# SyncE paces its expert weight loads: a granule's second transfer waits for the granule two places in front

## The reference

```python
def moe_swiglu(h, w_router, wg, wu, wd):
    logits = (h @ w_router).astype(jnp.float32)
    top_v, top_i = lax.top_k(logits, TOP_K)
    top_p = jax.nn.softmax(top_v, axis=-1)
    gates = jnp.sum(jax.nn.one_hot(top_i, N_EXPERTS, dtype=jnp.float32) * top_p[..., None], axis=-2)
    act = jax.nn.silu(jnp.einsum('bnd,edf->bnef', h, wg)) * jnp.einsum('bnd,edf->bnef', h, wu)
    act = act * gates.astype(h.dtype)[..., None]
    return jnp.einsum('bnef,efd->bnd', act, wd)
```

## Time and profile before

| | us |
|---|---|
| median of 3 runs | 1703.03 (1701.0 to 1705.19) |
| the profiled execution, its device time | 1703.7 |
| its span in the profile | 1701.9 |
| PE busy in the span | 1555.7 (91%) |
| SP's hardware queue | 195712 packets, 390.64 MB |
| mean traffic over the span | 254 GB/s |

### The profile page before, as it was taken

The page is one execution under the profiler, slowest core; times in us unless marked ns, Lnnn a source line. Parts: engine busy times, 40 slices in busy tenths (PEclk is TensorE's granted clock), DMA queues, the critical chain, the costliest instruction groups (busy, mean ns, idle before and its releaser), DMA issues.

```text
span 1701.9 us, 24840 instructions
## 1 busy us (share of the span) xinstructions
PE 1555.7 (91%) x9206; PEld 1034.7 (61%) x9207; DVE 760.2 (45%) x1236; ACT 555.3 (33%) x965; POOL 88.5 (5%) x109
## 2 busy tenths in 40 slices
PE   4798989999999799898878899999999989999795
PEld 1684567788888487467623577677566655655332
DVE  0483776433332655576610443333445534434225
ACT  0432454333332343361200333333244433334101
POOL 2010002200000011000100000000000000000002
PEclk8899999999999899999789999999999999999897
DMA  9245534944432623640999978887699999999992
GB/s 347 102 138 174 195 127 165 347 146 140 149 116 82 223 99 128 214 170 25 358 364 377 346 280 297 331 291 263 238 376 392 393 391 380 379 394 381 391 352 95
DMA packets 206624, 432.20 MB, mean 254 GB/s; under 512 B 11880, under 2 KB 52840, under 8 KB 206224
## 3 DMA queue, kind: packets, MB, share of 16 engines
q1 hardware_dynamic: 195712, 390.64, 63.3%
q0 software_dynamic: 7712, 29.05, 4.8%
q10 hardware_dynamic: 3056, 10.62, 1.8%
HBM read 409.55 MB, written 20.71 MB: 253 GB/s over the span
## 4 chain that ended last, share of the span: by engine, by line
issue 47%; PE 40%; DVE 6%; DMA 5%; ACT 2%; SPq 0%; POOL 0%; DVEq 0%; ACTq 0%; POOLq 0%
PE ps L2052 27%; PE ps L1984 3%; DMA small<-y_rows,row_at 2%; PE ps L2146 2%; DMA gu_ring<-in_w_ada 1%; PE ps L2111 1%; DMA d_ring<-in_w_ffn_down 1%; PE ps L2124 1%; PE ps L1987 1%; DVE gu_ring_parts L1320 1%; PE ps L1996 1%; PE ps L2008 1%; DVE smax L1412 1%; PE ps L2224 0%; PE ps L2598 0%
## 5 line engine op out<-in xcount | busy, mean ns | idle before, releaser
L2052 PE MATMUL ps<-d_ring_parts,scratch_parts 128*128 128x512 f32 (+1 forms) x444 | 171.8, 387 | 14.0 <-DVE hT_parts L1326 9.2
L2454 PE MATMUL ps<-ring,hT 128*64 128x512 f32 (+1 forms) x512 | 113.0, 585 | 19.1 <-issue 10.9
L2052 PE MATMUL ps<-gu_ring_parts,scratch_parts 128*128 128x512 f32 (+1 forms) x336 | 128.6, 383 | 0.0
L2052 PE MATMUL ps<-d_ring_parts,hT_parts 128*128 128x512 f32 (+1 forms) x312 | 119.2, 382 | 0.0
L2460 PE MATMUL ps<-ring,hT 128*32 128x256 f32 x1760 | 116.4, 382 | 3.0 <-issue 1.5
L1873 DVE TENSOR_TENSOR cst<-cst,ps 128x256 f32<-128x256 f32 (+2 forms) x89 | 32.7, 368 | 193.0 <-ACT cst L1159 193.0
L1184 ACT ACTIVATE qkv_parts<-ring 128x1024 fp32r<-128x1024 f32 x102 | 103.1, 1050 | 13.1 <-issue 13.1
L2052 PEld LDWEIGHTS ps<-d_ring_parts,scratch_parts 128*128 128x128 f32 x444 | 84.7, 191 | 32.2 <-issue 9.3
L2052 PE MATMUL ps<-gu_ring_parts,o_parts 128*128 128x512 f32 x264 | 103.3, 391 | 0.0
L1167 ACT ACTIVATE cst<-ps 128x128 f32<-128x128 f32 (+1 forms) x51 | 16.0, 315 | 235.3 <-PE ps L2476 225.9
L2454 PEld LDWEIGHTS ps<-ring,hT 128*64 128x64 f32 x512 | 36.1, 144 | 83.2 <-issue 68.4
(11 more groups left out here) (403 smaller groups left out, 3147.3 us busy)
## 6 DMA issues: line engine op xcount, KB each, us to landing
ring<-in_w_moe_gate SPq DMA_DIRECT2D x176, 512.0 KB, 10.4
ring<-in_w_moe_up SPq DMA_DIRECT2D x176, 512.0 KB, 11.3
ring<-in_w_moe_down SPq DMA_DIRECT2D x176, 512.0 KB, 10.0
gu_ring<-in_w_ada SPq DMA_DIRECT2D x48, 1024.0 KB, 7.4
gu_ring<-in_w_in SPq DMA_DIRECT2D x16, 1024.0 KB, 7.2
gu_ring<-in_w_ffn_gate SPq DMA_DIRECT2D x11, 1024.0 KB, 5.5
gu_ring<-in_w_ffn_up SPq DMA_DIRECT2D x11, 1024.0 KB, 8.1
d_ring<-in_w_ffn_down SPq DMA_DIRECT2D x11, 1024.0 KB, 10.0
```

The source lines that it names most:

```text
L2052: ins = pe.matmul(out, a, w, start=(start and n == 0), stop=(stop and n == 2))
L2454: ins = pe.matmul(ps[64 * j:64 * j + 64, bank, 0:2 * f].rearrange("p (a f) -> p a f", a=2), hT[:, kc, col:col + 64], wt[:, :, f * j:f * j ...
```

## The change

`IN_FLIGHT` is 2. In the loop, the first transfer of granule `pos` is issued as before; the second is issued only when granule `pos - 2` has landed in full (for `pos` 0 and 1 that is granule 31 or 32 of the turn before). In front of the loop, a granule's first transfer already waits for the granule two places earlier in the order of issue, and that order is written out in the list `first`; the waits for `ada_expanded` and `stored` stay where they were in it.

```diff
+IN_FLIGHT = 2
...
-            def load_granule(experts, pos):
+            def load_granule(experts, pos, pace=lambda: None):
...
                                      ).then_inc(landed, 16)
+                        if a == 0:
+                            pace()
...
                         sp.dma_start(half_view(ring, pos, f), w_moe_down[0, e][r0:r0 + P, :]).then_inc(landed, 16)
+                        if f == 0:
+                            pace()
...
+            def paced(t, pos, ahead=0):
+
+                if pos >= IN_FLIGHT:
+                    sp.wait_ge(ring_landed[pos - IN_FLIGHT], t * 32 + (32 * ahead + 32))
+                else:
+                    sp.wait_ge(ring_landed[pos - IN_FLIGHT + GRANULES], t * 32 + 32 * ahead)
+
+            first = list(range(1, 10)) + [0] + list(range(10, AHEAD))
             sp.wait_ge(out_mm, 12)
-            for pos in range(1, 10):
-                load_granule((0, 0), pos)
-            sp.wait_ge(ada_expanded, 32)
-            load_granule((0, 0), 0)
-            sp.wait_ge(stored, 128)
-            for pos in range(10, AHEAD):
+            for n, pos in enumerate(first):
+                if n >= IN_FLIGHT:
+                    sp.wait_ge(ring_landed[first[n - IN_FLIGHT]], 32)
+                if pos == 0:
+                    sp.wait_ge(ada_expanded, 32)
+                if pos == 10:
+                    sp.wait_ge(stored, 128)
                 load_granule((0, 0), pos)
...
                     freed(t, pos - AHEAD)
-                    load_granule(now, pos)
+                    load_granule(now, pos, lambda: paced(t, pos))
...
                     freed(t, pos + GRANULES - AHEAD)
-                    load_granule(then, pos)
+                    load_granule(then, pos, lambda: paced(t, pos, 1))
...
                 freed(NE - 1, pos - AHEAD)
-                load_granule(now, pos)
+                load_granule(now, pos, lambda: paced(NE - 1, pos))
```

## The result

The changed kernel takes 1715.74 us (median of 6 runs, 1710.56 to 1727.42) where the kernel before took 1702.01 us beside it (1696.62 to 1705.19). The ratio is 1.0099, with a 95% interval of 1.0071 to 1.0126. The forecast was 1703.5 us in a range up to 1711, with 0.16 for slower. So it was wrong, and the rival that names bubbles in the load stream was the one that came. The profiled execution has a span of 1716.5 us against 1701.9.

What follows compares the result with a forecast made beforehand. PE and the load stream were taken to bound the expert phase in turn. 1703.7 + 0 (SP instructions) + 0 (queue depth) + 0.5 (SP pauses) = 1704.2, less 0.7 for this execution: 1703.5 us, range 1696.5 to 1711; nothing measurable 0.72.

Steps and rivals of the forecast that it cites:

- the rival that names bubbles in the load stream: Second transfers in the stretches that count lose time: 0.1 us a granule gives 1710 us, 0.4 gives 1728; chance 0.16.
- What bounds the kernel: Expert phase: PE bounds 1000 to 1226 us; elsewhere the transfer engines are never out of work, DMA share 0.94 to 1.04.
- Instructions on SP: New waits in SP's issue stream, at most about 0.2 us each: SP needs 1.34 us of a granule's 2.71, cost nothing.
- The depth of the queue: At a second transfer's release, three transfers (4.05 us) cover 2.65 us of start, completion and wait: cost nothing.
- the rival's "for": Argument for bubbles: the 16 engines don't finish together, so the cover of 4.05 us is thinner for all but the slowest.
- The row on which the zero rested: Ring transfer issued at 1179.09 with three on their way landed 1.4 us behind the one before: taken as no loss.
- How many granules count: A delay moves PE only in 885 to 923 (some 13 granules) and 1226 to 1369 (some 49): 62 granules.
- The hiding: Last stretch: PE waits 5.3 us for DVE behind POOL's chain of gathers, so the first few us of delay are hidden.
- SP's pauses: Top of a turn, SP loads table values for 3.05 us: 0.3 us too much at about two places, 0.5 us in all.
- In front of the loop: Stricter pace, 2.7 us of cover against 2.65; a loss of some us by 881 is hidden by the hole there.
- The other queues: ACT's and POOL's transfers and code fetches get quicker: five gathers gain 1.55 us each, 7.8 us, 1696 us; chance 0.12.
- What would show it: Ring landings of 5 to 7 us, no long SP issues, about 387 GB/s; wrong if GB/s fall by 2% or more.

Runs made afterwards that it cites:

- All waits with none binding: The changed kernel with IN_FLIGHT 8 instead of 2, so every wait is executed and none holds anything back: 1701.98 us, ratio 1.0005.
- one ahead: The changed kernel with IN_FLIGHT 1, so one transfer is on its way when a landing lets the next go: 1989.91 us, ratio 1.1693.
- 3 ahead: The change itself against the kernel before: three transfers are on their way when a landing lets the next go; 1715.74 us, ratio 1.0099.
- two ahead: The changed kernel, IN_FLIGHT 2, wait moved in front of both transfers, so two are on their way at a release: 1762.58 us, ratio 1.0362.
- five: The changed kernel with IN_FLIGHT 3, wait still between the two transfers, so five are on their way at a release: 1700.57 us, ratio 0.9992.
- four ahead: The changed kernel, IN_FLIGHT 3, wait moved in front of both transfers, so four are on their way at a release: 1702.89 us, ratio 1.0013.
- the run with every third granule: The changed kernel, but only every third granule waits two places back, the others three: 1709.12 us, ratio 1.0051.

## Why the prediction was wrong

**What bounds the kernel** was read rightly. The two limits, and where each rules, are the same after, and the loss came through the stream in the stretches with a DMA share near 1.

**Instructions on SP: right.** All waits with none binding gave a ratio of 1.0005.

**The depth of the queue: the step that failed.** The forecast set the cover of 4.05 us against 2.65 us and took nothing. The 2.65 us hold for the slowest of the 16 engines, and one ahead shows it (median 3.9 us a granule against 4.0 by this sum). But the others are up to 1.9 to 2.9 us in front, so they run out of work with 3 ahead. The forecast named this in the rival's "for" and set it aside with "the slowest engine, which sets the landings, always has its three transfers". That would be enough if an engine that runs out simply gave up its lead. The packets show that it doesn't: some of those that follow a moment with too little under way take up to ten times the usual 84 ns. If I add the lead to what must fit, the sum is 2.65 + 1.9 to 2.9 = 4.6 to 5.6 us. Three ahead (4.05) and two (2.7) lose, five (6.75) don't, and four (5.4) stand on the edge and lose nothing that can be measured. That is what the table shows. The step from lead to slow packets is read from the traces; no run changed the lead by itself, so it is argued and not shown alone. It fits the table, but it doesn't say why most granules lose nothing with three ahead; the instruction transfers, which take about 1 us on their queue, are a likely part of that, untested. Nor does it fit the run with every third granule. Shown is that the depth costs it: from one ahead to four the loss falls in every step, at four and five it can't be told from none, and the waits alone cost nothing that can be told.

The row on which the zero rested, the start at 1179.09, was a single one. It was read by its landing, the time of the slowest engine, which can't show what the others lost. That the row "shows none of it" was a misreading: right behind that issue the traffic falls to 188 GB/s in the kernel before as well (windows of 1 us, GB/s last).

```profile
1180.00:1181.00 1.00, 1.00 (x11) 0.37 (x9) 0.00 (x0) 0.00 (x0) 0.00 (x0) 1.00 0.81 188
1181.00:1182.00 1.00, 1.00 (x11) 0.56 (x12) 0.00 (x0) 0.94 (x2) 0.00 (x0) 1.00 0.99 371
```

In 1180.0 to 1180.25 only 10.6 packets are under way on average, and ring packets of 2048 bytes take up to 835 ns. The dip and the long packets were there to be seen before the change was run.

The Trainium skill ("DMA: Bandwidth & Descriptors", Latency and other measured facts) has HBM access at 0.2 us on average and 2 us at high load. The forecast weighed that and let the row decide. The estimate from it was 0.4 us for each of 62 granules, 25 us. Measured are 2.84 - 2.71 = 0.13 us for each, and none of it steadily. So it had the sign right where my zero didn't, and was about as far off in size: 1728 and 1703.5 us, where 1715.7 came. Whether the HBM's latency has a part in the loss no run here shows.

**How many granules count: also wrong.** The forecast counted 62 and held the last stretch to be hidden. The stream from 1226 us on to its end is 149 granules with no stop but what PE asks for, and 149 x 0.13 = 19 us; the same granules took 436.5 us before (issue of the first to landing of the last, PE's holds included) and 455.7 us after. I had looked for the place where PE waited already. But a stream that only just keeps up has no waits until its store is used up: PE waits 7.1 us at L2474 by 1372, nothing for the ring from there to 1607, and 19.1 us behind 1610. The hiding itself was right: with the last turn alone paced nothing was lost. But the cover was 5.3 us, and what came due was more than three times that. The threshold of the rival, 0.08 us a granule, was worked out with 62; with 149 and 5.3 us of cover it is some (5.3 + 5.1) / 149 = 0.07 us. So the count mattered little for the sign, and much for the size: 62 x 0.13 = 8 us would have been 1712; 149 granules less the cover, 19.4 - 5.3 = 14 us, give 1717 from the forecast's 1703, where 1716 came. That this sum comes out so near is in part luck. In the two profiles the last landing comes 22.9 us later: 19.3 from this stream, and 3.6 that were there when it started. From the last landing to the end of the span it is 39.2 us before and 30.9 after, so 8.3 us were hidden and not 5.3, which leaves the 14.6 by which the spans differ.

**SP's pauses: the term was nearly right for where it stood, and missed one place.** At the top of a turn (`pos` 16) the second transfer is issued 0.32 to 0.35 us after its release, where the forecast had 0.3. Among the last 149 granules two others are late once the stream has started, both in the last turn:

```profile
1666.26 0.38 SPq L725 DMA_DIRECT2D ring<-in_w_moe_gate  x1
1672.02 0.39 SPq L725 DMA_DIRECT2D ring<-in_w_moe_up  x1
1672.61 0.37 SPq L725 DMA_DIRECT2D ring<-in_w_moe_gate  x1
```

The releasing landing was at 1667.92, so SP came 4.1 us late. In this gap the queues show an 8 KB transfer of the kind "instruction" at 1670.21. The two granules behind it took 6.4 and 6.0 us, and PE waited 6.2 us for the first. The kernel before has the same pause, from 1641.99 to 1647.39, and the deep queue hid it: its granules there took 2.96 and 2.9 us. Other runs have it too, at the same granule or the next. The stream loses 6.4 + 6.0 - 2 x 2.7 = 7.0 us by it in this execution. Its price at the end was not measured: with the last turn not paced the median is 2.3 us lower, which the intervals (1.0047 to 1.0092 against 1.0071 to 1.0126) don't tell from none, and in that profile too a pause of SP (5.3 us) and the ring transfer behind it stand near the end of the chain that ended last. That the pause is an instruction fetch is read from the transfer in the gap, not shown.

**In front of the loop:** the forecast held any loss by 881 hidden by the hole there. In the time this can't be told from right (ratio 1.0018, 0.9996 to 1.0041). In the profiles it wasn't hidden: the last stream starts some 5 us later wherever the front is paced by 2.

**The other queues: nothing that can be told.** ACT's stores of 512 KB from `qkv` land in 3.9 us (median) instead of 5.2, but there are only four of them, and in the other profiles with three ahead in the loop it is 4.6 and 5.1. The gathers' median is 7.2 instead of 7.5, far from the 1.55 us each that the rival asked for, and the other profiles with three ahead have 6.9 and 7.8.

**What would show it** served well: landings of 5 to 7 us and short issues came as said, and the first sign named for an error, GB/s down by 2% or more, is the one that came.

## What to carry to other kernels

If you hold transfers back until earlier ones have landed, don't count the cover at the landing. A landing is the slowest engine's; the fastest is ahead of it by some us (1.9 to 2.9 here), and by the reading above that comes on top of start and completion. Here 512 KB transfers wanted four ahead, and three cost 5% of the rate. Before you cost a slower stream, find the whole stretch in which it runs without a hole and multiply by all of its granules; its waits come due at the end of it, not where they stand today. And a deep queue hides more than latency: also the pauses of the engine that feeds it, and, by the traces here, the instruction transfers beside it. When you rest a cost of nothing on one row, look at the traffic of that microsecond too, and not only at the landing.

## What was not expected of the hardware

- A load stream with three 512 KB transfers on their way doesn't slow down evenly. The median granule stays at 2.67 us, and one in seven (17 of 118) takes 3.2 to 4.4 us with no transfer of ACT's beside it.
- Granules near a 16 KB instruction transfer take 3.12 us on average with three transfers ahead, and 2.69, like all others, in the deep queue of the kernel before.
- Packets of 2048 bytes, 84 ns in the median, take up to 891 ns in the place shown, most often just after moments in which fewer than the usual 16 or 17 packets are under way. With one ahead such packets cost 25.6 us of 200 for each engine, with no pace 3.3.
- The 16 engines' parts of one transfer end 2.1 to 3.1 us apart in a queue that isn't held (2.9 in the kernel before), 1.8 to 2.0 us with three ahead at every release.
- The DMA share says little near 1: 1.04 at 387 GB/s, 1.02 at 369, and still 0.98 at 348 with two ahead.
